# A two-layer decoder trunk on one core: 96 seats in place of 128 in each pass of the expert layer

## The chip, the core and the metric

The kernel runs on 1 core of one Trainium2 chip. The metric is the device time of the whole program, in microseconds (us); lower is better. All inputs and weights are float32 in HBM.

## What is computed

Two decoder layers act on 256 tokens of width 1024. Each has a token mixer (an RWKV-7 group, a short convolution and a dilated attention group behind one projection, then an output projection) and a feed-forward part. The feed-forward part of layer 0 is a dense SwiGLU; that of layer 1 sends each token to 2 of 8 experts of inner width 3584. Cut to what matters here:

```python
SEQ = 256; D_MODEL = 1024; D_FF = 3584; N_EXPERTS = 8; TOP_K = 2
def moe_swiglu(h, router, wg, wu, wd):
    logits = xt @ router
    topv, topi = lax.top_k(logits, TOP_K)
    gates = jax.nn.softmax(topv, axis=-1)
    ...
    # every expert e, for the tokens that chose it:
    #   out[token] += gate * ((silu(x @ wg[e]) * (x @ wu[e])) @ wd[e])
```

## The kernel before, in words

Layer 0, its dense feed-forward part and the mixers of layer 1 come first; the change doesn't touch them. The expert layer is `moe_pass(p)`, which each engine has in its own version: SP (weights), POOL (rows of tokens), PE, ACT and DVE.

**Seats.** Routing gives each token a rank within each of its two experts. A pass has 128 seats for each expert (P = 128): pass 0 serves ranks 0 to 127. DVE sets `flag` when an expert has more tokens than seats (L2468), and each engine ends with a branch on `flag` behind which `moe_pass(1)` stands (L1528 on PE). An empty seat has token 0 and gate 0. At the start of an expert its tokens' rows are gathered from HBM into `x_slots` (L726, POOL, an indirect DMA), turned by eight transposes (`turn_slots`, L1427) and split into a high and a low part, `xg_hi` and `xg_lo`. Expert 0 has a gather by products instead (`gather`, L770).

**Split products.** The products run in float32r, so each float32 product is three: high x high, high x low, low x high (`three`, L789 to L791). The tokens are the stationary operand, 128 rows of the inner dimension by the seats; the weights are the moving operand, 512 columns at a time. Weights arrive by SP's DMAs of 1 MB into a ring of 6 slots. ACT rounds a piece of 1024 columns to `w_hi` (L1543), DVE makes the rest, `w_lo` (L2246); there are four pieces of buffer, and PE frees a piece after six products (`pc_free`).

**Order.** The inner width is walked in 7 chunks of 512 (NJ = 7). For a chunk: gate product into bank 0 or 1 (8 steps of the width), up product into bank 2 or 3 (8 steps), SiLU on ACT (L1911), multiply on DVE (L2505), four transposes on PE (`turn`, L1464), which write bank 6, a copy to `at_hi` on ACT (L1543) and a subtraction to `at_lo` on DVE (L2509), and the down product into banks 4 and 5 (8 steps). That is 24 steps of three products, 72 products a chunk, 7 chunks, 8 experts: 4032 products, 224 transposes of `turn`, and 56 of `turn_slots` for experts 1 to 7. The order is written by hand and fixed: on PE the turn of chunk j - 1 stands between the gate and the up product of chunk j. Experts 0 to 6 are one loop body, expert 7 stands apart. After an expert ACT scales the result by the gates (`yg`, L1940), and POOL adds the rows to `out` in HBM by an indirect DMA (L732); the last expert does so in two halves (L740), and the program ends when the second has landed.

```python
def turn(j, at1):                                     # PE, L1459
    for i in range(4):
        last_ = pe.transpose(bank[6][:, i * P:(i + 1) * P], act_b[j % 2][:, i * P:(i + 1) * P], ident)
```

In a transpose the data are the stationary operand and the identity is the moving one. The mixers' matmuls (L770, L1105) and the transposes are in float32, not float32r.

Of the kernel before, what the change touches and what calls it, by code (L numbers as in the profile page):

```python
# [35 lines left out]
SLOTS = 6  # L36
FIRST_OVER = 4
# [79 lines left out]
def decoder_trunk(nc, x, consts, masks, params, lora, vres_v2, w_in, w_o, dense_wg, dense_wu, dense_wd,  # L117
                  router, gains, moe_wg, moe_wu, moe_wd, h_rows, out):
    with ExitStack() as ctx:
# [29 lines left out]
        xg_hi, xg_lo = (a[:, 0:KT * P] for a in (acts_hi, acts_lo))  # L149
        at_hi, at_lo = (a[:, KT * P:KT * T].rearrange("p (b n) -> p b n", b=2) for a in (acts_hi, acts_lo))  # L150
# [445 lines left out]
        def _(sp):  # L596
# [66 lines left out]
            with sp.If(over_full > 0):  # L663
                moe_pass(1)
# [3 lines left out]
        def _(pool):  # L668
# [52 lines left out]
            def moe_pass(p):  # L721
                def take_rows(e, at1):
                    pool.wait_ge(ga_done, at1 * 2)
                    pool.tensor_copy(from_row[:, :], slot_token[:, e, :]).then_inc(from_set, 1)
                    pool.wait_ge(from_set, at1 - p)
                    pool.indirect_dma_start(x_slots, None, h_rows,  # L726
                                            bass.IndirectOffsetOnAxis(from_row[:, :], 0)).then_inc(slots_in, 16)

                def add_rows(e, at1):
                    pool.wait_ge(to_set, at1 + 1)  # L730
                    pool.wait_ge(yg_kept, at1 * 2 + 2)
                    pool.indirect_dma_start(out, bass.IndirectOffsetOnAxis(to_row[:, :], 0), yg, None,  # L732
                                            compute_op=ALU.add).then_inc(rows_out, 16)
# [12 lines left out]
                pool.wait_ge(index_ready, p + 1)  # L746
                pool.tensor_copy(to_row[:, :], slot_token[:, 0, :]).then_inc(to_set, 1)
                for e in range(NE - 1):
                    take_rows(e + 1, p * NE + e + 1)
                    add_rows(e, p * NE + e)  # L750
                    if e + 2 < NE:
                        pool.tensor_copy(to_row[:, :], slot_token[:, e + 1, :]).then_inc(to_set, 1)
                    else:
                        pool.tensor_copy(to_half[0][:, :], slot_half[:, 0:1])
                        pool.tensor_copy(to_half[1][:, :], slot_half[:, 1:2]).then_inc(to_set, 1)
                add_halves(p * NE + NE - 1)
# [6 lines left out]
            with pool.If(over_full > 0):  # L763
                moe_pass(1)
# [3 lines left out]
        def _(pe):  # L768
# [641 lines left out]
            def moe_pass(p):  # L1410
                def slot_pairs(e):

                    if e == 0:
                        pe.wait_ge(pairs_ready, p + 1)
                    for b in range(2):
                        last_ = mm(bank[7][:, 4 * e:4 * e + 4], onehot[b][:, e, :], token_gate[:, b, e, :],
                                   b == 0, b == 1)
# [12 lines left out]

                def gather(e, at1):

                    for f in range(2):
                        if p == 0:
                            pe.wait_ge(ht_ready, f + 1)
                        for i in range(4):
                            k = 4 * f + i
                            for b in range(2):
                                last_ = mm(bank[1 + 2 * f][:, i * P:(i + 1) * P], h_tok[:, b, k * P:(k + 1) * P],
                                           onehot[b][:, e, :].bitcast(F32) if p else hot_first[:, b, :], b == 0, b == 1)  # L1440
                        last_.then_inc(ga_done, 1)

                def column_chunk(kind, j, at1):
                    if j >= 2:
                        pe.wait_ge(ac_ready, at1 * NJ + (j - 1))
                    b = bank[(0 if kind == "g" else 2) + j % 2]
                    for q in range(4):

                        pe.wait_ge(lo_ready, at1 * PIECES_E + (MOE0 + 4 * place_of[(kind, j)] + q + 1))
                        if kind == "g" and j == 0 and q % 2 == 0:  # L1450
                            pe.wait_ge(ga_low, at1 * 2 + (q // 2 + 1))
                        for i in range(2):
                            k = 2 * q + i
                            ks, cs = slice(k * P, (k + 1) * P), slice(i * CW, (i + 1) * CW)
                            last_ = three(b[:, :], xg_hi[:, ks], xg_lo[:, ks], w_hi[:, q, cs], w_lo[:, q, cs],
                                          k == 0, k == KT - 1)
                        last_.then_inc(pc_free, 1)

                def turn(j, at1):  # L1459
# [3 lines left out]
                    for i in range(4):  # L1463
                        last_ = pe.transpose(bank[6][:, i * P:(i + 1) * P], act_b[j % 2][:, i * P:(i + 1) * P],  # L1464
                                             ident)
                    last_.then_inc(at_done, 1)

                def down_half(j, q, hf):
                    ks, cs = slice(q * P, (q + 1) * P), slice(hf * CW, (hf + 1) * CW)
                    return three(bank[4 + hf][:, :], at_hi[:, j % 2, ks], at_lo[:, j % 2, ks],  # L1470
                                 w_hi[:, q, cs], w_lo[:, q, cs], j == 0 and q == 0, j == NJ - 1 and q == 3)
# [56 lines left out]
            with pe.If(over_full > 0):  # L1528
                moe_pass(1)
# [3 lines left out]
        def _(act):  # L1533
# [366 lines left out]
            def moe_pass(p):  # L1900
                def gathered(at1):
                    for f in range(2):
                        act.wait_ge(ga_done, at1 * 2 + (f + 1))
                        copy(xg_hi[:, f * CW:(f + 1) * CW], bank[1 + 2 * f][:, :]).then_inc(ga_kept, 1)

                def silu(j, at1):
# [4 lines left out]
                    act.activation(sil_b[j % 2], bank[j % 2][:, :], ACT.Silu).then_inc(sl_done, 1)  # L1911

                def turned(j, at1):
                    act.wait_ge(at_done, at1 * NJ + (j + 1))
                    copy(at_hi[:, j % 2, :], bank[6][:, :]).then_inc(at_kept, 1)

                def expert(e, at1, last_one):
# [17 lines left out]
                    for hf in range(2):  # L1935
                        if last_one and hf == 0:
                            act.wait_ge(half_done, p + 1)
                        if last_one and hf:
                            act.wait_ge(pc_free, at1 * PIECES_E + (MOE0 + PIECES_E + PIECES))
                        act.activation(yg[:, hf * 512:(hf + 1) * 512], bank[4 + hf][:, :], ACT.Identity,  # L1940
                                       scale=gate_e).then_inc(yg_kept, 1)
# [19 lines left out]
            with act.If(over_full > 0):  # L1961
                moe_pass(1)
# [4 lines left out]
        def _(dve):  # L1967
# [490 lines left out]
            def finish_ranks():  # L2458
# [9 lines left out]
                TS(flag[:, :], cmax, float(P), None, ALU.is_gt).then_inc(flag_ready, 1)  # L2468
# [15 lines left out]
            def moe_pass(p):  # L2484
# [7 lines left out]
                def gathered(at1, halves_=range(2)):  # L2492
                    for f in halves_:
                        dve.wait_ge(ga_kept, at1 * 2 + (f + 1))
                        fs = slice(f * CW, (f + 1) * CW)
                        TT(xg_lo[:, fs], bank[1 + 2 * f][:, :], xg_hi[:, fs].bitcast(F32), ALU.subtract).then_inc(
                            ga_low, 1)

                def multiply(j, at1):
# [5 lines left out]
                    TT(act_b[j % 2], sil_b[j % 2], bank[2 + j % 2][:, :], ALU.mult).then_inc(ac_ready, 1)  # L2505

                def turned(j, at1):
                    dve.wait_ge(at_kept, at1 * NJ + (j + 1))
                    TT(at_lo[:, j % 2, :], bank[6][:, :], at_hi[:, j % 2, :].bitcast(F32), ALU.subtract).then_inc(  # L2509
                        at_low, 1)  # L2510

                def expert(e, at1, last_one):
# [11 lines left out]
                    dve.tensor_copy(gate_e, slot_gates[:, e, :]).then_inc(gate_ready, 1)  # L2524
# [12 lines left out]
                if p:  # L2537
                    then(TS(rank, rank, -float(P), None, ALU.add))
# [14 lines left out]
                pairs = bank[7][:, 0:4 * NE].rearrange("p (e n) -> p e n", e=NE)  # L2553
                for hf in range(2):
                    TS(slot_half[:, hf:hf + 1], pairs[:, NE - 1, 0:1], 2.0, float(hf), ALU.mult, ALU.add)
                dve.tensor_copy(slot_token[:, :, 0], pairs[:, :, 0]).then_inc(index_ready, 1)
                then(dve.tensor_copy(slot_gates[:, :, 0], pairs[:, :, 1]))
                then(TT(slot_gates[:, :, 0], slot_gates[:, :, 0], pairs[:, :, 2], ALU.add))
# [7 lines left out]
            with dve.If(over_full > 0):  # L2566
                moe_pass(1)
# [48 lines left out]
```

## Time and profile before

| | us |
|---|---|
| median of 3 runs | 1574.8 (1573.14 to 1574.96) |
| span of the profiled execution, first to last instruction | 1570.8 |
| of it before the expert layer's first product (L789 at 612.18) | 612 |
| PE busy / weight loads / DVE / ACT / POOL | 1555.2 / 1360.4 / 1264.9 / 1073.6 / 81.0 |
| read from HBM | 438.63 MB, of it 336 transfers of 1 MB for the experts |
| granted TensorE clock, mean | 0.996 of 2.4 GHz |

The profiled execution's own time is not among the figures; its span is 4.0 us below the median of the runs. PE is matmul time and PEld the weight loads, which lie beside it. Since matmuls are pipelined, the records of two that follow each other overlap; what counts is the distance from start to start.

### The profile page before, as it was taken

The page shows a single profiled execution, that of the slowest core. Times are in us where ns is not written, and L with a number is a line of the kernel's source. Part 1 is how long each engine was busy: PE and PEld are TensorE (multiplying, and loading weights), DVE is VectorE, ACT ScalarE, POOL GpSimd, SP SyncE. Part 2 cuts the span into 40 slices and gives each one's busy share as a digit, 9 for nine tenths or more (in the row PEclk, how much of TensorE's full clock was granted, in tenths as well). Part 3 has the DMA queues.
Part 4 walks back from the last instruction along what each step waited for, and adds up shares of the span by engine and source line. Part 5 has one row for each costly group of instructions (what it writes and reads, how often), then busy time and mean ns, then how long its engine had stood idle before and what let it go on. Part 6 is the DMA issues. An engine that isn't in the chain of part 4 may idle for free.

```text
span 1570.8 us, 28731 instructions
## 1 busy us (share of the span) xinstructions
PE 1555.2 (99%) x10958; PEld 1360.4 (87%) x10958; DVE 1264.9 (81%) x1448; ACT 1073.6 (68%) x1323; POOL 81.0 (5%) x82
## 2 busy tenths in 40 slices
PE   9999999999999999999999999999999999999998
PEld 8989999999999898888888888888888888888886
DVE  5686654444567877999999999999999999999996
ACT  5545444444446455888888888888888888888885
POOL 0022000000000400000000000000000000000000
PEclk9999999999999999999999999999999999999999
DMA  8700655555445008999999999999999999999994
GB/s 314 235 2 3 220 192 180 187 188 185 126 158 158 3 19 321 389 379 360 396 387 348 397 393 359 397 391 354 397 390 353 397 391 356 394 386 366 389 380 162
DMA packets 189944, 447.76 MB, mean 285 GB/s; under 512 B 8208, under 2 KB 10784, under 8 KB 189728
## 3 DMA queue, kind: packets, MB, share of 16 engines
q1 hardware_dynamic: 186480, 434.46, 75.7%
q0 software_dynamic: 2688, 9.44, 2.8%
q10 hardware_dynamic: 688, 2.62, 0.5%
q8 instruction: 63, 1.03, 0.3%
q14 instruction: 25, 0.20, 0.0%
HBM read 438.63 MB, written 6.29 MB: 283 GB/s over the span
## 4 chain that ended last, share of the span: by engine, by line
PE 95%; DVE 3%; ACT 1%; issue 1%; DMA 0%; POOL 0%; SPq 0%; ACTq 0%; DVEq 0%; POOLq 0%
PE bank L789 27%; PE bank L791 27%; PE bank L790 27%; PE bank L770 9%; PE bank L1464 2%; DVE w_lo L2246 1%; ACT w_hi L1543 0%; DMA ring<-in_w_in 0%; PE bank L960 0%; PE bank L810 0%; PE bank L1427 0%; PE bank L1213 0%; PE bank L1105 0%; DVE w_lo L1985 0%; POOL out L740 0%
## 5 line engine op out<-in xcount | busy, mean ns | idle before, releaser
L1543 ACT ACTIVATE w_hi<-ring 128x1024 fp32r<-128x1024 f32 x812 | 858.4, 1061 | 330.1 <-PE bank L791 319.9
L2246 DVE TENSOR_TENSOR w_lo<-ring,w_hi 128x1024 fp32r<-128x1024 f32 x672 | 813.7, 1224 | 60.4 <-ACT w_hi L1543 11.3
L789 PE MATMUL bank<-w_hi,acts_hi 128*128 128x512 f32 (+1 forms) x1376 | 539.0, 392 | 0.4 <-DVE w_lo L2246 0.3
L791 PE MATMUL bank<-w_hi,acts_lo 128*128 128x512 f32 (+1 forms) x1376 | 533.1, 387 | 0.0
L790 PE MATMUL bank<-w_lo,acts_hi 128*128 128x512 f32 (+1 forms) x1376 | 532.3, 387 | 0.0
L791 PEld LDWEIGHTS bank<-w_hi,acts_lo 128*128 128x128 f32 x1376 | 258.3, 188 | 53.7
L789 PEld LDWEIGHTS bank<-w_hi,acts_hi 128*128 128x128 f32 x1376 | 258.6, 188 | 52.1 <-DVE w_lo L2246 1.4
L790 PEld LDWEIGHTS bank<-w_lo,acts_hi 128*128 128x128 f32 x1376 | 258.7, 188 | 50.6
L789 PE MATMUL bank<-acts_hi,w_hi 128*128 128x256 f32 x884 | 252.4, 286 | 1.8 <-DVE acts_lo L2175 0.8
L790 PE MATMUL bank<-acts_lo,w_hi 128*128 128x256 f32 x884 | 250.1, 283 | 0.0
L791 PE MATMUL bank<-acts_hi,w_lo 128*128 128x256 f32 x884 | 250.1, 283 | 0.0
L2237 DVE TENSOR_TENSOR w_lo<-ring,w_hi 128x1024 fp32r<-128x1024 f32 x84 | 102.7, 1225 | 110.8 <-ACT w_hi L1543 110.8
L789 PEld LDWEIGHTS bank<-acts_hi,w_hi 128*128 128x128 f32 x884 | 169.5, 192 | 5.8 <-issue 3.9
L790 PEld LDWEIGHTS bank<-acts_lo,w_hi 128*128 128x128 f32 x884 | 169.6, 192 | 0.0
L791 PEld LDWEIGHTS bank<-acts_hi,w_lo 128*128 128x128 f32 x884 | 169.5, 192 | 0.0
L1985 DVE TENSOR_TENSOR w_lo<-ring,w_hi 128x1024 fp32r<-128x1024 f32 x40 | 48.1, 1220 | 30.9 <-ACT w_hi L1543 30.9
L770 PE MATMUL bank<-arena 64*64 64x128 f32 (+10 forms) x718 | 68.9, 295 | 2.7 <-DVE arena L2452 1.3
L1543 ACT ACTIVATE arena<-bank 128x256 f32<-128x256 f32 (+4 forms) x67 | 30.0, 485 | 57.0 <-PE bank L770 28.4
L770 PEld LDWEIGHTS bank<-arena 64*64 64x64 f32 (+6 forms) x718 | 50.6, 154 | 13.2 <-issue 4.4
L789 PE MATMUL bank<-da_hi,w_hi 128*128 128x256 f32 x192 | 54.3, 283 | 0.0
L790 PE MATMUL bank<-da_lo,w_hi 128*128 128x256 f32 x192 | 54.3, 283 | 0.0
L791 PE MATMUL bank<-da_hi,w_lo 128*128 128x256 f32 x192 | 54.3, 283 | 0.0
(247 smaller groups left out, 1115.9 us busy)
## 6 DMA issues: line engine op xcount, KB each, us to landing
ring<-in_moe_wg SPq DMA_DIRECT2D x112, 1024.0 KB, 6.8
ring<-in_moe_wu SPq DMA_DIRECT2D x112, 1024.0 KB, 7.0
ring<-in_moe_wd SPq DMA_DIRECT2D x112, 1024.0 KB, 6.8
ring<-in_w_in SPq DMA_DIRECT2D x24, 1024.0 KB, 7.5
ring<-in_dense_wg SPq DMA_DIRECT2D x14, 1024.0 KB, 5.2
ring<-in_dense_wu SPq DMA_DIRECT2D x14, 1024.0 KB, 5.2
ring<-in_dense_wd SPq DMA_DIRECT2D x14, 1024.0 KB, 4.9
ring<-in_w_o SPq DMA_DIRECT2D x8, 1024.0 KB, 7.5
```

The costliest lines, as they stand in the source:

```text
L770: return pe.matmul(out_, lhsT, rhs, start=start, stop=stop)
L789: pe.matmul(out_, a_hi, b_hi, start=first, stop=False, **kw)
L790: pe.matmul(out_, a_hi, b_lo, start=False, stop=False, **kw)
L791: return pe.matmul(out_, a_lo, b_hi, start=False, stop=final, **kw)
L1464: last_ = pe.transpose(bank[6][:, i * P:(i + 1) * P], act_b[j % 2][:, i * P:(i + 1) * P], ident)
L1543: return act.activation(o, i, ACT.Copy, **kw)
L1985: TT(w_lo[:, q, :], ring[:, slot_of[n], q % 2 * PIECE:(q % 2 + 1) * PIECE], w_hi[:, q, :].bitcast(F32), ALU.subtract).then_inc(lo_ready, 1)
L2237: TT(w_lo[:, q, :], ring[:, slot_of[n], q % 2 * PIECE:(q % 2 + 1) * PIECE], w_hi[:, q, :].bitcast(F32), ALU.subtract).then_inc(lo_ready, 1)
L2246: TT(w_lo[:, q, :], raw, w_hi[:, q, :].bitcast(F32), ALU.subtract).then_inc(lo_ready, 1)
```

## The change

Seats become 96 (`SEATS`), and `PASSES = -(-256 // 96) = 3`: behind the flag stand passes 1 and 2 in place of pass 1. The threshold of the flag follows. All tiles that have the seats as their free dimension (`xg`, `at`, the transposes' outputs) shrink from 128 to 96 columns a block; those that have them as partitions (`bank` 0 to 5, `sil_b`, `act_b`, `yg`) are used on partitions 0 to 95. POOL gathers and adds 96 rows an expert. The order of the work is the same. Cut to its core (hunks that say the same for another engine or tile are left out):

```diff
+SEATS = 96
+PASSES = -(-T // SEATS)
...
-        xg_hi, xg_lo = (a[:, 0:KT * P] for a in (acts_hi, acts_lo))
+        xg_hi, xg_lo = (a[:, 0:KT * SEATS] for a in (acts_hi, acts_lo))
...
             with pe.If(over_full > 0):
-                moe_pass(1)
+                for p in range(1, PASSES):
+                    moe_pass(p)
...
                     pool.indirect_dma_start(out.rearrange("t (h d) -> (t h) d", h=2),
-                                            bass.IndirectOffsetOnAxis(to_half[hf][:, :], 0),
-                                            yg[:, hf * CW:(hf + 1) * CW], None,
+                                            bass.IndirectOffsetOnAxis(to_half[hf][rows, :], 0),
+                                            yg[rows, hf * CW:(hf + 1) * CW], None,
...
-                            last_ = pe.transpose(bank[1 + 2 * f][:, i * P:(i + 1) * P], x_slots[:, k * P:(k + 1) * P],
-                                                 ident)
+                            last_ = pe.transpose(bank[1 + 2 * f][:, i * SEATS:(i + 1) * SEATS],
+                                                 x_slots[0:SEATS, k * P:(k + 1) * P], ident[0:SEATS, 0:SEATS])
...
-                            ks, cs = slice(k * P, (k + 1) * P), slice(i * CW, (i + 1) * CW)
-                            last_ = three(b[:, :], xg_hi[:, ks], xg_lo[:, ks], w_hi[:, q, cs], w_lo[:, q, cs],
+                            ks, cs = slice(k * SEATS, (k + 1) * SEATS), slice(i * CW, (i + 1) * CW)
+                            last_ = three(b[0:SEATS, :], xg_hi[:, ks], xg_lo[:, ks], w_hi[:, q, cs], w_lo[:, q, cs],
...
-                        last_ = pe.transpose(bank[6][:, i * P:(i + 1) * P], act_b[j % 2][:, i * P:(i + 1) * P],
-                                             ident)
+                        last_ = pe.transpose(bank[6][:, i * SEATS:(i + 1) * SEATS],
+                                             act_b[j % 2][0:SEATS, i * P:(i + 1) * P], ident[0:SEATS, 0:SEATS])
...
-                    copy(at_hi[:, j % 2, :], bank[6][:, :]).then_inc(at_kept, 1)
+                    copy(at_hi[:, j % 2, :], bank[6][:, 0:4 * SEATS]).then_inc(at_kept, 1)
...
-                TS(flag[:, :], cmax, float(P), None, ALU.is_gt).then_inc(flag_ready, 1)
+                TS(flag[:, :], cmax, float(SEATS), None, ALU.is_gt).then_inc(flag_ready, 1)
...
-                    TT(act_b[j % 2], sil_b[j % 2], bank[2 + j % 2][:, :], ALU.mult).then_inc(ac_ready, 1)
+                    TT(act_b[j % 2][0:SEATS, :], sil_b[j % 2][0:SEATS, :], bank[2 + j % 2][0:SEATS, :],
+                       ALU.mult).then_inc(ac_ready, 1)
...
-                    TT(at_lo[:, j % 2, :], bank[6][:, :], at_hi[:, j % 2, :].bitcast(F32), ALU.subtract).then_inc(
+                    TT(at_lo[:, j % 2, :], bank[6][:, 0:4 * SEATS], at_hi[:, j % 2, :].bitcast(F32), ALU.subtract).then_inc(
```

The instructions of the executed path keep their places. The first turn in the expert loop, between a gate and an up product, reads so on PE before (the size is that of the output, partitions by columns):

```order
3678 L791 MATMUL bank<-w_hi,acts_lo 128x512
3679 L1460 ISA
3680 L1464 MATMUL bank<-arena 128x128 x4
3681 L1449 REGISTER_ALU
3682 L789 MATMUL bank<-w_hi,acts_hi 128x512
```

and now:

```order
3678 L797 MATMUL bank<-w_hi,acts_lo 96x512
3679 L1467 ISA
3680 L1471 MATMUL bank<-arena 128x96 x4
3681 L1456 REGISTER_ALU
3682 L795 MATMUL bank<-w_hi,acts_hi 96x512
```

The products keep their 512 columns and lose 32 output partitions; the four transposes lose 32 of 128 columns. PE has 7032 rows in all in place of 5879; all the added ones stand behind the branch on the flag, as the second further pass.

## Rows read from the trace of the kernel before

**Rows 1.** The page: busy time, and the span in 40 slices.

```profile
PE 1555.2 (99%) x10958; PEld 1360.4 (87%) x10958; DVE 1264.9 (81%) x1448; ACT 1073.6 (68%) x1323; POOL 81.0 (5%) x82
...
PEclk9999999999999999999999999999999999999999
```

**Rows 2.** Busy time by stretch (us; x: instructions; then granted clock, DMA share, GB/s).

```profile
135.00:140.00 5.00, 5.00 (x159) 4.87 (x159) 1.90 (x9) 3.46 (x8) 0.00 (x0) 1.00 0.00 0
300.00:400.00 100.00, 100.00 (x836) 100.00 (x835) 49.79 (x44) 42.69 (x44) 0.00 (x0) 1.00 0.55 183
800.00:900.00 100.00, 100.00 (x458) 82.82 (x457) 93.41 (x86) 82.00 (x88) 5.64 (x4) 1.00 1.03 374
```

**Rows 3.** The waits, window 700 to 1500 us: who waited for whom, total, times, longest.

```profile
ACT w_hi L1543 <- PE bank L791: 139.7, 484, 0.4
DVE w_lo L2246 <- ACT w_hi L1543: 9.2, 21, 0.9
```

**Rows 4.** PE in order of time, around the turn at 800 us.

```profile
799.97 0.39 PE L791 MATMUL bank<-w_hi,acts_lo 128*128 128x512 f32 x1
800.20 0.60 PE L1464 MATMUL bank<-arena 128*128 128x128 f32 x4
800.55 0.48 PE L789 MATMUL bank<-w_hi,acts_hi 128*128 128x512 f32 x1
800.87 0.39 PE L790 MATMUL bank<-w_lo,acts_hi 128*128 128x512 f32 x1
...
805.88 0.39 PE L791 MATMUL bank<-w_hi,acts_lo 128*128 128x512 f32 x1
```

**Rows 5.** Groups by form, PE: stationary rows*columns, moving rows x columns, count, busy, mean ns.

```profile
L790 PE MATMUL bank<-w_lo,acts_hi 128*128 128x512 f32 x1344 | 523.2, 389 | 0.0
L790 PE MATMUL bank<-acts_lo,w_hi 128*128 128x256 f32 x884 | 250.1, 283 | 0.0
L1464 PE MATMUL bank<-arena 128*128 128x128 f32 x224 | 33.5, 271 | 0.0
L770 PE MATMUL bank<-arena,ring 128*128 128x256 f32 x128 | 29.3, 383 | 0.0
L1105 PE MATMUL bank<-spare,arena 64*64 64x64 f32 x72 | 3.8, 221 | 0.0
```

**Rows 6.** Groups by form, weight loads of 128 and of 64 columns.

```profile
L790 PEld LDWEIGHTS bank<-w_lo,acts_hi 128*128 128x128 f32 x1376 | 258.7, 188 | 50.6
L1464 PEld LDWEIGHTS bank<-arena 128*128 128x128 f32 x224 | 28.0, 140 | 7.1
L770 PEld LDWEIGHTS bank<-arena 64*64 64x64 f32 x408 | 14.4, 132 | 2.1 <-issue 1.1 <-ACT arena L1543 0.7
```

**Rows 7.** In order of time, start of the expert layer: copy, subtraction, gather.

```profile
608.59 3.84 PE L770 MATMUL bank<-arena 128*128 128x128 f32 x32 [1.29 <-DVE arena L2452]
...
610.68 0.60 ACT L1543 ACTIVATE acts_hi<-bank 128x512 fp32r<-128x512 f32 x1 [2.96 <-PE bank L770]
611.30 0.69 DVE L2496 TENSOR_TENSOR acts_lo<-bank,acts_hi 128x512 fp32r<-128x512 f32 x1 [0.31 <-ACT acts_hi L1543]
...
618.07 0.50 PE L789 MATMUL bank<-w_hi,acts_hi 128*128 128x512 f32 x1 [0.16 <-DVE w_lo L2246]
```

**Rows 8.** Groups of the page: the two splits of a weight piece.

```profile
L1543 ACT ACTIVATE w_hi<-ring 128x1024 fp32r<-128x1024 f32 x812 | 858.4, 1061 | 330.1 <-PE bank L791 319.9
L2246 DVE TENSOR_TENSOR w_lo<-ring,w_hi 128x1024 fp32r<-128x1024 f32 x672 | 813.7, 1224 | 60.4 <-ACT w_hi L1543 11.3
```

**Rows 9.** In order of time, POOL's last issue.

```profile
1564.60 1.55 POOL L740 DMA_INDIRECT out<-arena,to_half  x1 [0.59 <-ACT arena L1940]
```

**Rows 10.** DMA: GB/s in 40 slices, and time to landing of an up half and of the last rows.

```profile
GB/s 314 235 2 3 220 192 180 187 188 185 126 158 158 3 19 321 389 379 360 396 387 348 397 393 359 397 391 354 397 390 353 397 391 356 394 386 366 389 380 162
...
ring<-in_moe_wu SPq DMA_DIRECT2D x112, 1024.0 KB, 7.0
...
out<-arena,to_half POOLq DMA_INDIRECT x2, 4.8
```

More of the change, by code:

```diff
@@ L148, in decoder_trunk @@
         h_hi, h_lo = (a[:, :].rearrange("p (k t) -> p k t", k=KT) for a in (acts_hi, acts_lo))
-        xg_hi, xg_lo = (a[:, 0:KT * P] for a in (acts_hi, acts_lo))
-        at_hi, at_lo = (a[:, KT * P:KT * T].rearrange("p (b n) -> p b n", b=2) for a in (acts_hi, acts_lo))
+        xg_hi, xg_lo = (a[:, 0:KT * SEATS] for a in (acts_hi, acts_lo))
+        at_hi, at_lo = (a[:, KT * P:KT * P + KT * SEATS].rearrange("p (b n) -> p b n", b=2) for a in (acts_hi, acts_lo))
         class Region:
@@ L721, in moe_pass @@
             def moe_pass(p):
+                rows = slice(0, min(SEATS, T - p * SEATS))
                 def take_rows(e, at1):
                     pool.wait_ge(ga_done, at1 * 2)
-                    pool.tensor_copy(from_row[:, :], slot_token[:, e, :]).then_inc(from_set, 1)
+                    pool.tensor_copy(from_row[0:SEATS, :], slot_token[0:SEATS, e, :]).then_inc(from_set, 1)
                     pool.wait_ge(from_set, at1 - p)
-                    pool.indirect_dma_start(x_slots, None, h_rows,
-                                            bass.IndirectOffsetOnAxis(from_row[:, :], 0)).then_inc(slots_in, 16)
+                    pool.indirect_dma_start(x_slots[rows, :], None, h_rows,
+                                            bass.IndirectOffsetOnAxis(from_row[rows, :], 0)).then_inc(slots_in, 16)
                 def add_rows(e, at1):
@@ L731, in add_rows @@
                     pool.wait_ge(yg_kept, at1 * 2 + 2)
-                    pool.indirect_dma_start(out, bass.IndirectOffsetOnAxis(to_row[:, :], 0), yg, None,
+                    pool.indirect_dma_start(out, bass.IndirectOffsetOnAxis(to_row[rows, :], 0), yg[rows, :], None,
                                             compute_op=ALU.add).then_inc(rows_out, 16)
@@ L763, in _ @@
             with pool.If(over_full > 0):
-                moe_pass(1)
+                for p in range(1, PASSES):
+                    moe_pass(p)
         @block.tensor
@@ L1438, in gather @@
                             for b in range(2):
-                                last_ = mm(bank[1 + 2 * f][:, i * P:(i + 1) * P], h_tok[:, b, k * P:(k + 1) * P],
-                                           onehot[b][:, e, :].bitcast(F32) if p else hot_first[:, b, :], b == 0, b == 1)
+                                last_ = mm(bank[1 + 2 * f][:, i * SEATS:(i + 1) * SEATS], h_tok[:, b, k * P:(k + 1) * P],
+                                           onehot[b][:, e, 0:SEATS].bitcast(F32) if p else hot_first[:, b, 0:SEATS],
+                                           b == 0, b == 1)
                         last_.then_inc(ga_done, 1)
@@ L1528, in _ @@
             with pe.If(over_full > 0):
-                moe_pass(1)
+                for p in range(1, PASSES):
+                    moe_pass(p)
         @block.scalar
@@ L1903, in gathered @@
                         act.wait_ge(ga_done, at1 * 2 + (f + 1))
-                        copy(xg_hi[:, f * CW:(f + 1) * CW], bank[1 + 2 * f][:, :]).then_inc(ga_kept, 1)
+                        copy(xg_hi[:, f * 4 * SEATS:(f + 1) * 4 * SEATS], bank[1 + 2 * f][:, 0:4 * SEATS]).then_inc(ga_kept, 1)
                 def silu(j, at1):
@@ L1939, in expert @@
                             act.wait_ge(pc_free, at1 * PIECES_E + (MOE0 + PIECES_E + PIECES))
-                        act.activation(yg[:, hf * 512:(hf + 1) * 512], bank[4 + hf][:, :], ACT.Identity,
-                                       scale=gate_e).then_inc(yg_kept, 1)
+                        act.activation(yg[0:SEATS, hf * 512:(hf + 1) * 512], bank[4 + hf][0:SEATS, :], ACT.Identity,
+                                       scale=gate_e[0:SEATS, :]).then_inc(yg_kept, 1)
                     if not last_one:
@@ L1961, in _ @@
             with act.If(over_full > 0):
-                moe_pass(1)
+                for p in range(1, PASSES):
+                    moe_pass(p)
         @block.vector
@@ L2494, in gathered @@
                         dve.wait_ge(ga_kept, at1 * 2 + (f + 1))
[L2495 to L2496 removed]
+                        fs = slice(f * 4 * SEATS, (f + 1) * 4 * SEATS)
+                        TT(xg_lo[:, fs], bank[1 + 2 * f][:, 0:4 * SEATS], xg_hi[:, fs].bitcast(F32), ALU.subtract).then_inc(
                             ga_low, 1)
@@ L2537, in moe_pass @@
                 if p:
-                    then(TS(rank, rank, -float(P), None, ALU.add))
+                    then(TS(rank, rank, -float(SEATS), None, ALU.add))
                     place_tokens()
@@ L2552, in moe_pass @@
                 dve.wait_ge(pairs_done, p + 1)
-                pairs = bank[7][:, 0:4 * NE].rearrange("p (e n) -> p e n", e=NE)
+                pairs = bank[7][0:SEATS, 0:4 * NE].rearrange("p (e n) -> p e n", e=NE)
                 for hf in range(2):
[L2555 to L2558, printed above, removed]
+                    TS(slot_half[0:SEATS, hf:hf + 1], pairs[:, NE - 1, 0:1], 2.0, float(hf), ALU.mult, ALU.add)
+                seats = slice(0, SEATS)
+                dve.tensor_copy(slot_token[seats, :, 0], pairs[:, :, 0]).then_inc(index_ready, 1)
+                then(dve.tensor_copy(slot_gates[seats, :, 0], pairs[:, :, 1]))
+                then(TT(slot_gates[seats, :, 0], slot_gates[seats, :, 0], pairs[:, :, 2], ALU.add))
                 dve.wait_ge(index_ready, p + 1)
@@ L2566, in _ @@
             with dve.If(over_full > 0):
-                moe_pass(1)
+                for p in range(1, PASSES):
+                    moe_pass(p)
 _OUT = "out"
```

18 lines of the change are left out of this document (9 added, 9 removed).

## The prediction

> **What bounds the kernel now.** I read the page first [rows 1]: PE is busy 99% of the span, the other engines less, and its clock stands at 2.4 GHz but for moments. A busy PE is not yet a PE at its pace, so I next took the stretches [rows 2]: inside the expert layer PE starts 458 matmuls in 100 us, and DVE and ACT are busy 93 and 82 of the 100. Then the waits [rows 3]: in 800 us of expert layer no row has PE waiting for anybody. ACT waits 139.7 us for PE to free a piece of buffer, DVE 9.2 us for ACT. So PE sets the pace, and the splits of the weights follow it.
>
> The order of time around one turn [rows 4] gives PE's own distances. From 800.87 to 805.88 lie 22 steps from start to start, 0.227 us each, of which 512 columns at 2.4 GHz are 213 ns. In the dense part [rows 2] 836 matmuls of 256 columns take 100 us, 120 ns each, of which 107 are columns. Both have 13 to 14 ns beside their columns, a fixed amount. Check: a chunk is 72 products at 0.227 = 16.34 us plus a turn. The turn costs 800.20 to 800.55 for the four transposes, and the second product after it starts 0.32 after the first in place of 0.227: 0.35 + 0.09 = 0.44 us. That is 16.8 us a chunk, 117.5 an expert; with eight transposes of the rows (0.9) 118.4, eight times 947 us, and 612 before it: 1559 of the 1570.8. The rest is the end.
>
> **The change part by part.**
>
> *Does a further pass run?* Only if an expert has over 96 tokens. This is a question of data, not of the profile: the reference's routing of the given inputs puts 53, 55, 65, 74, 56, 60, 86 and 63 tokens on the eight experts. The largest is 86, so the flag stays 0, as with 128 seats, and passes 1 and 2 are code that is skipped by the same single branch as before.
>
> *The 4032 products.* They keep 512 moving columns and lose 32 stationary ones. What shrinks is the weight load: 188 ns for 128 columns, 132 for 64 [rows 6], 0.87 ns a column, so some 160 ns for 96. It was hidden below the 227 ns already, and it stays hidden. The columns' 213 ns stay. Only the fixed 13.6 ns could depend on the stationary columns, and no float32r row of this trace has fewer than 128. The bounds: gone altogether, 4032 x 13.6 = -55 us; in proportion to the columns, 13.6 x 3/4, -3.4 x 4032 = -13.7 us; upwards a third, +4.5 x 4032 = +18 us. I take **0**: the amount is the same with 256 and 512 moving columns and in both parts of the program, which looks like a cost of each matmul, not of what it holds.
>
> *The 224 transposes of turn.* Here the moving operand is the identity, and it shrinks from 128 to 96 columns; the stationary operand, the data, keeps 128 columns and loses 32 rows. What does the distance of 109 ns between two of them hang on ([rows 4]: 0.60 us for four less the last one's 0.271 [rows 5] is 0.329 for three steps)? If on the moving side, it is 128 columns at two cycles of 2.4 GHz, 107 ns. The durations speak for it. Plain float32 matmuls of 64 and 256 moving columns last 221 and 383 ns, 0.84 ns a column, which is two cycles; float32r products of 256 and 512 last 283 and 389, 0.41 ns a column, one cycle [rows 5]. At 128 columns the first line gives 275 ns, the second 230. A transpose lasts 271, so it streams at two cycles. The transposes' loads are also 48 ns shorter than the products' at the same 128 columns, 140 against 188 [rows 6], so a load is not what they wait for. Then 32 columns less are 32 x 0.83 = 26.7 ns each, 107 ns a turn, and **224 x 0.0267 = -6.0 us**. If on the load, it is 0; that is the other bound. I take the first.
>
> A rule bears on this. The Trainium skill, "TensorE: Matmul & The Clock Gate", sections "Back-to-back issue gap" and "LDWEIGHTS (loading the stationary operand)", has a warm matmul cost its moving columns / 2.4 GHz + 2.5 ns, whatever the stationary side, and a load its stationary columns / 1.2 GHz, whatever the rows. By it the products gain nothing, but a transpose would be 56 ns of moving columns behind a load of 107 ns that this change leaves alone, so the -6.0 and the -1.5 below would be 0; it is the first rival.
>
> *The 56 transposes of the rows* (turn_slots) are the same form, 8 for each of experts 1 to 7: 56 x 0.0267 = **-1.5 us**, bound 0. All these lie in PE's own line, where nobody else is waited for, so each ns comes off the end.
>
> *The first gather* is 32 matmuls in 3.84 us [rows 7], some 0.115 us apart, more than 107 of moving columns at two cycles: by load, which stays. 0; bound -0.8 us (32 x 26.7 ns).
>
> *Copies and subtractions.* ACT's copy of turned data takes 0.60 us for 512 columns against 1.06 for 1024 [rows 7, 8], 0.90 ns a column; 128 fewer save 0.12. DVE's subtraction: 0.69 against 1.22, 1.04 ns a column, saves 0.13. In mid-layer they lie beside PE, whose waits are nil [rows 3]; they are worth 0 there and make the splits' room a little wider. At the start PE does wait for them: the first product needs copy and subtraction, and at 618.07 PE waits for DVE, whose line holds two subtractions. 0.12 + 2 x 0.13 = **-0.4 us**. At the last chunk PE waits for DVE again, behind ACT's copy: **-0.1 us**. SiLU, multiply and the scaling work on fewer partitions but the same 512 columns; 0.
>
> *The end.* The last thing is POOL's issue of the second half of the last rows, 1.55 us [rows 9], and its landing, 4.8 us [rows 10], both for 128 rows. If the issue scales with rows, 96 save 0.39; if it is fixed, 0. The landing in proportion would save 1.2, fixed 0. I take **-0.4** for both. The other gathers and adds lie behind 107 us of an expert; 0.
>
> *The weights.* PE goes from 118.4 to 117.4 us an expert (7 x 0.107 + 8 x 0.027). The transfers then need 44.04 MB in 117.4 us, 375 GB/s over 372. Slices with 397 stand in the trace [rows 10], an up half lands after 7.0 us where a slot's turn of six is over 16 us, so nothing becomes late. DVE's 93 of 100 becomes about 93.6: it is next in line but not reached.
>
> **Sum**: -6.0 - 1.5 - 0.4 - 0.1 - 0.4 = -8.4 us, 1562.4 of span. The span is 4.0 below the median of the runs, and what lies around it doesn't change: 1574.8 - 8.4 = **1566.4 us**, 0.5% faster.
>
> **The rivals.**
>
> 1. *The transposes wait for their loads*, 128 stationary columns before and after. For it: 109 ns is also what 128 columns at 0.83 ns take, and two explanations fit one number. Against it: the two-cycle duration, the shorter load of 140 ns, and the gather, which is load-bound and slower at 0.115. Then only -0.9 remains: 1573.9, not to be told from no change.
>
> 2. *The fixed 13.6 ns shrink with the stationary columns*, to three quarters: a further -13.7 us, 1552.7. For it: the trace doesn't say what they are, and a handing over of 128 columns would fit. Against it: nothing direct. A small part of it, 1 ns a product, would already be -4 us.
>
> 3. *Slower: the step from one stationary set to the next gets longer when the set isn't a full 128 columns.* Its place is the start of each of the 4032 products. It decides from 8.4 / 4032 = 2.1 ns a product on; if the 13.6 ns rise by a third, +18 us gives 1584.5. Against it: the float32 matmuls on 64 stationary columns lie on one line of duration with those on 128 [rows 5], the transposes too, and the 160 ns load has 67 ns of room. The Trainium skill, same page, section "Weight-path perf modes", says that the fast weight load is on only with exactly 128 weights and a type other than float32, which would be lost at 96. The products' loads show no fast mode that could be lost: the 64 columns between 132 and 188 ns take 0.87 ns each, one cycle of 1.2 GHz.
>
> 4. *A further pass runs after all*, if the routing on the chip gave an expert over 96 tokens: from 612 to the end is a pass of 950 us, so over 2500 us. With 86 tokens at most, it would need ten tokens to change expert.
>
> 5. *The clock falls*, since three quarters of the array's columns work. The stretch of 64x64 matmuls at 135 us, a quarter of the array, was granted 1.00 [rows 2]. A chance too small to count.
>
> **How the numbers follow.** A measurement of this kernel can tell about 0.2%, 3.1 us, from no change. Forecast 0.65, with a range of its own from 1563 to 1569 (landing and gather at either bound, a few tenths of a ns on the products); rival 1 0.13; rival 2 0.13, some of it as a small part; rival 3 0.08; rivals 4 and 5 together 0.01. Faster: 0.65 + 0.13 = 0.78; same 0.13; slower 0.09. The range holds the forecast, rival 1 up to 1575 and the part of rival 2 up to 1.3 ns a product (another -5.4 us): **1561 to 1575**. It leaves out the rest of rival 2 and all of 3 and 4.
>
> **What the changed profile would show.** Four transposes in 0.49 us in place of 0.60, and each lasting about 244 ns in place of 271. Products still 0.227 apart, with loads of some 160 ns. A chunk of 16.7 us. No row of PE waits inside the layer. The copy at 0.48 and the subtraction at 0.55 us. POOL's last issue at 1.2 to 1.55 us. Products at another distance than 0.227 by over 1 ns make the prediction wrong, in either direction; so do transposes still 109 ns apart.

## The result, and the profile after

| | us |
|---|---|
| before, median of 5 runs | 1574.8 (1572.98 to 1575.24) |
| changed kernel, median of 5 runs | 1580.13 (1579.69 to 1583.82) |
| ratio over all runs, 95% interval | 1.0044 (1.0031 to 1.0057) |
| span of the profiled executions, before and after | 1570.8, 1581.3 |
| forecast | 1566.4 (1561 to 1575) |

The kernel became slower: the median rose by 5.3 us (0.34%), and the ratio, which is taken over all runs and not from the two medians, is 1.0044 (0.44%), where 0.5% faster was forecast. The profiled execution was the slowest of the five (1583.82), with the granted clock at 0.59 of full speed from 608 to 616 us, at the first gather; the spans of the other four are 1577.3 to 1579.5.

The page of the changed kernel, busy time and weight loads, answering to [rows 1] and [rows 8]:

```profile
PE 1565.2 (99%) x10958; PEld 1249.5 (79%) x10958; DVE 1256.0 (79%) x1448; ACT 1065.7 (67%) x1323; POOL 83.6 (5%) x82
...
L2255 DVE TENSOR_TENSOR w_lo<-ring,w_hi 128x1024 fp32r<-128x1024 f32 x672 | 814.5, 1223 | 77.6 <-ACT w_hi L1551 60.9
```

PE runs the same 10958 instructions: no further pass ran. Weight loads take 111 us less, DVE and ACT 8 to 9 less, PE 10 more. The stretch 900 to 1000 us, first of the kernel before, then of the changed one (columns as in [rows 2]):

```profile
900.00:1000.00 100.00, 100.00 (x458) 82.82 (x457) 93.39 (x87) 81.94 (x88) 4.21 (x4) 1.00 1.04 381
```

```profile
900.00:1000.00 100.00, 100.00 (x454) 70.38 (x453) 91.41 (x85) 80.51 (x87) 4.40 (x4) 1.00 1.03 372
```

454 matmuls in place of 458, at the full clock in both. DVE and the transfers are less busy, so neither has become the bound. The waits of the changed kernel, 700 to 1500 us, against [rows 3]:

```profile
ACT w_hi L1551 <- PE bank L797: 152.7, 480, 0.4
...
DVE w_lo L2255 <- ACT w_hi L1551: 54.2, 292, 0.9
```

Again no row has PE waiting. ACT waits longer for PE, and DVE longer for ACT: all follow a slower PE. PE in order of time at a turn, against [rows 4]:

```profile
803.70 0.39 PE L797 MATMUL bank<-w_hi,acts_lo 128*96 128x512 f32 x1
803.93 0.49 PE L1471 MATMUL bank<-arena 96*128 96x96 f32 x4
804.21 0.45 PE L795 MATMUL bank<-w_hi,acts_hi 128*96 128x512 f32 x1
804.50 0.39 PE L796 MATMUL bank<-w_lo,acts_hi 128*96 128x512 f32 x1
...
806.12 0.40 PE L797 MATMUL bank<-w_hi,acts_lo 128*96 128x512 f32 x1
```

The four transposes take 0.49 us, as forecast. But from 804.50 to 806.12 there are seven steps of 0.231 us, where the kernel before has 0.227. Single distances tell more. In the kernel before, the distance after the first product of a turn is about 316 ns, the next nine or so are 224 to 236, and then they settle to a strict 227, 226, 227. In the changed kernel they never settle; they go on, nearly all between 228 and 236. Over some 3300 distances between products from 700 to 1500 us, without the long one after each turn, the mean is 227.3 before and 231.5 after.

That closes the account. An expert, from its first row transpose to that of the next, took 118.57 us and takes 119.71, 1.14 more. Its 504 products cost 504 x 4.2 = +2.1; its seven turns, 0.67 us before and 0.57 now from the first transpose to the second product, give back 0.7, and the eight row transposes 0.2, together 1.2. The first expert, from its first product to the row transposes of the next, takes 114.9 us in both traces: +2.0 for its 480 products, less 0.7 for its turns, 0.4 for a wait near 618 us that is gone, and 0.7 for a group of 16 small matmuls near 624 us. The other seven take 7.9 us more, and the end is 0.3 shorter: +7.6 us. The other 2.9 of the 10.5 us between the two spans stand before the first product, 2.8 of them at the first gather, where the clock fell in this execution and not in that of the kernel before. The medians differ by less, 5.3, since four of the five runs of the changed kernel had mean clocks of 0.997 and 0.998. The 35 runs of the kernel before that were timed beside the experiments had 0.995 as their median, and from 0.998 to 0.994 their time rises by 1.2 us for each 0.001. At 0.998 the three runs of the changed kernel, 1579.7 to 1580.1 us, stand 8 us above the one run of the kernel before, 1571.5.

### The profile page after: what moved, and what is told of

Same layout as the page of the kernel before. It is cut to its first block, busy times and chain, and to the rows that moved or that the text cites. A ratio compares the mean times of both kernels' runs of the same rounds, so it can differ in the third digit from the quotient of the medians.

```text
span 1581.3 us, 28731 instructions
## 1 busy us (share of the span) xinstructions
PE 1565.2 (99%) x10958; PEld 1249.5 (79%) x10958; DVE 1256.0 (79%) x1448; ACT 1065.7 (67%) x1323; POOL 83.6 (5%) x82
## 4 chain that ended last, share of the span: by engine, by line
PE 96%; DVE 2%; ACT 1%; issue 1%; DMA 0%; POOL 0%; SPq 0%; DVEq 0%; ACTq 0%; POOLq 0%
PE bank L795 28%; PE bank L797 28%; PE bank L796 27%; PE bank L776 9%; PE bank L1471 1%; ACT w_hi L1551 0%; DMA ring<-in_w_in 0%; PE bank L966 0%; PE bank L816 0%; PE bank L1433 0%; PE bank L1219 0%; DVE w_lo L1994 0%; PE bank L1111 0%; POOL out L745 0%; ACT arena L1551 0%
## 5 line engine op out<-in xcount | busy, mean ns | idle before, releaser
L795 PE MATMUL bank<-w_hi,acts_hi 128*96 128x512 f32 (+1 forms) x1376 | 541.4, 393 | 0.2 <-DVE w_lo L2255 0.2
L797 PE MATMUL bank<-w_hi,acts_lo 128*96 128x512 f32 (+1 forms) x1376 | 539.4, 392 | 0.0
L796 PE MATMUL bank<-w_lo,acts_hi 128*96 128x512 f32 (+1 forms) x1376 | 536.4, 390 | 0.0
L797 PEld LDWEIGHTS bank<-w_hi,acts_lo 128*96 128x96 f32 (+1 forms) x1376 | 222.8, 162 | 94.1
L796 PEld LDWEIGHTS bank<-w_lo,acts_hi 128*96 128x96 f32 (+1 forms) x1376 | 223.5, 162 | 90.9
L795 PEld LDWEIGHTS bank<-w_hi,acts_hi 128*96 128x96 f32 (+1 forms) x1376 | 223.0, 162 | 89.6 <-DVE w_lo L2255 1.0
L796 PE MATMUL bank<-acts_lo,w_hi 128*128 128x256 f32 x884 | 250.1, 283 | 0.0
L796 PEld LDWEIGHTS bank<-acts_lo,w_hi 128*128 128x128 f32 x884 | 169.6, 192 | 0.0
L776 PE MATMUL bank<-arena 64*64 64x128 f32 (+11 forms) x718 | 72.0, 300 | 3.2 <-DVE arena L2461 1.3
L796 PE MATMUL bank<-da_lo,w_hi 128*128 128x256 f32 x192 | 54.3, 283 | 0.0
```

The costliest lines, as they stand in the source:

```text
L776: return pe.matmul(out_, lhsT, rhs, start=start, stop=stop)
L795: pe.matmul(out_, a_hi, b_hi, start=first, stop=False, **kw)
L796: pe.matmul(out_, a_hi, b_lo, start=False, stop=False, **kw)
L797: return pe.matmul(out_, a_lo, b_hi, start=False, stop=final, **kw)
```

## The experiments

The theories: A, the distance of the products depends on how many columns the stationary operand has; B, the short transposes keep PE out of step; C, it is where the blocks begin, every 96 columns (384 bytes) in place of 128.

**e1_wide_loads.** The changed kernel with blocks 128 columns apart, of which 96 are seats and 32 hold leftovers, and products on all 128. Cut to the gate and up products; the down product changes likewise, and the copies and subtractions write their 96 columns into the wider blocks:

```diff
-                            ks, cs = slice(k * SEATS, (k + 1) * SEATS), slice(i * CW, (i + 1) * CW)
-                            last_ = three(b[0:SEATS, :], xg_hi[:, ks], xg_lo[:, ks], w_hi[:, q, cs], w_lo[:, q, cs],
+                            ks, cs = slice(k * P, (k + 1) * P), slice(i * CW, (i + 1) * CW)
+                            last_ = three(b[:, :], xg_hi[:, ks], xg_lo[:, ks], w_hi[:, q, cs], w_lo[:, q, cs],
```

Expected: 

> The change, but the products' stationary operand has 128 columns again (96 seats and 32 columns of leftovers, blocks 128 apart); transposes, copies and subtractions stay at 96. Theory A (the products' distance depends on the number of stationary columns): products 0.227 apart as before, transposes 82 ns apart, so 7.5 to 9 us below before, 1566 us, ratio 0.995. Theory B (the shorter transposes, or the rows left out in them, keep PE out of step afterwards): products stay 231.5 ns apart, about 1580 us. Theory C (where the blocks begin, every 384 bytes in the change): 0.227 here too; the next run tells C from A.

Measured: 1568.96 us (1564.51 to 1570.23), ratio 0.9965 (0.9952 to 0.9979). Mean distance of the products 227.1, and 82 ns from transpose to transpose. Theory B falls: the short transposes are all there, and the products settle again. PE in order of time, and the stretch 900 to 1000 us:

```profile
830.38 0.40 PE L805 MATMUL bank<-w_hi,acts_lo 128*128 128x512 f32 x1
830.61 0.49 PE L1479 MATMUL bank<-arena 96*128 96x96 f32 x4
830.89 0.47 PE L803 MATMUL bank<-w_hi,acts_hi 128*128 128x512 f32 x1
831.21 0.39 PE L804 MATMUL bank<-w_lo,acts_hi 128*128 128x512 f32 x1
```

```profile
900.00:1000.00 100.00, 100.00 (x461) 82.82 (x460) 93.12 (x87) 81.61 (x87) 3.37 (x4) 1.00 1.04 380
```

461 matmuls in 100 us. The turn is 0.59 us in the mean, against 0.67 before and 0.57 in the changed kernel. An expert takes 117.75 us, against 118.57 before.

**e2_held96, e2_held64, e2_held112, e6_held127.** The kernel before, where only the products' stationary columns are cut; HELD is 96, 64, 112, 127. Seats from HELD on are left out of the products; with 64 some of these hold tokens. The output partitions shrink with the stationary columns, so no run tells the two apart. Cut to the gate and up products, the down product changes likewise:

```diff
-                            ks, cs = slice(k * P, (k + 1) * P), slice(i * CW, (i + 1) * CW)
-                            last_ = three(b[:, :], xg_hi[:, ks], xg_lo[:, ks], w_hi[:, q, cs], w_lo[:, q, cs],
+                            ks, cs = slice(k * P, k * P + HELD), slice(i * CW, (i + 1) * CW)
+                            last_ = three(b[0:HELD, :], xg_hi[:, ks], xg_lo[:, ks], w_hi[:, q, cs], w_lo[:, q, cs],
```

Expected of 96: 

> The kernel before, with 96 of the 128 columns of each block as the products' stationary operand and 96 output partitions; all else as before, blocks 128 columns apart, transposes of 128. Seats 96 to 127, which are empty, are left out of the products. Theory A: products 231.5 ns apart, 4.2 ns x 4032 = 17 us slower, 1592 us, ratio 1.011. Theories B and C: 227 ns and 1575 us, no change.

Expected of 64: 

> As the last, with 64 stationary columns; seats from 64 on are left out of the products. Theory A has two forms. If any number below 128 puts PE out of step: 231 to 232 ns, span near 1587. If the cost grows with the columns missing: 4.2 ns for 32 is 8.4 for 64, 235.7 ns, span near 1605. Theories B and C: 227 ns.

Expected of 112: 

> As the last, with 112 stationary columns; seats 112 to 127, which are empty, are left out. Theory A, any number below 128: 231 to 232 ns, span near 1587. Theory A, in proportion: 2.1 ns more, 229.4 ns, span near 1579. Theories B and C: 227 ns.

Expected of 127: 

> The kernel before with 127 of 128 stationary columns in the products; seat 127, which is empty, is left out. Theory A as a step at 128: 230 to 231 ns between products, as with 112, 96 and 64, span near 1583. Theory A in proportion: 227.3 ns, span near 1571.

| stationary columns | mean distance, ns | weight load, ns | an expert, us | span, us |
|---|---|---|---|---|
| 64 | 229.9 | 134 | 119.89 | 1580.7 |
| 96 | 230.0 | 161 | 119.88 | 1586.6 |
| 112 | 230.4 | 175 | 120.06 | 1584.0 |
| 127 | 233.4 | 187 | 121.51 | 1596.4 |
| 128 (before) | 227.3 | 188 | 118.57 | 1570.8 |

Only the kernel with 96 was timed more than once: 1584.52 us (1582.35 to 1588.36), ratio 1.0059 (1.0043 to 1.0075). Its clock was 0.994 in the profiled execution, hence the span above that with 112. Theory A holds, as a step at 128 and not in proportion: one column less than 128 costs 6 ns a product, 16 less cost 3.1, 32 or 64 less 2.7. Never settling isn't what costs the time: with 127 columns the products do settle, to a strict 233, 233, 234. The stretch 900 to 1000 us with 96 and with 127, and the weight loads of 127 and of 64 columns, grouped by form, 700 to 1500 us:

```profile
900.00:1000.00 100.00, 100.00 (x453) 71.01 (x452) 92.45 (x86) 81.11 (x87) 3.73 (x4) 1.00 1.03 376
```

```profile
900.00:1000.00 100.00, 100.00 (x448) 80.51 (x447) 91.33 (x84) 80.18 (x86) 4.08 (x4) 1.00 1.02 370
```

```profile
L791 PEld LDWEIGHTS bank<-w_lo,acts_hi 128*127 128x127 f32 x1106 | 207.0, 187 | 48.8
```

```profile
L791 PEld LDWEIGHTS bank<-w_lo,acts_hi 128*64 128x64 f32 x1121 | 150.7, 134 | 101.0
```

453 matmuls with 96 columns and 448 with 127. The load's own record knows no step: 134, 161, 175, 187, 188 ns is a straight line of 0.84 ns a column. The products' records do know it. Their durations grow nearly as much as their distances; the same product, by its mean duration (the last number but one) with 128, with 96 in the changed kernel, and with 127, 700 to 1500 us:

```profile
L790 PE MATMUL bank<-w_lo,acts_hi 128*128 128x512 f32 x1134 | 441.5, 389 | 0.0
```

```profile
L796 PE MATMUL bank<-w_lo,acts_hi 128*96 128x512 f32 x1123 | 440.6, 392 | 0.0
```

```profile
L791 PE MATMUL bank<-w_lo,acts_hi 128*127 128x512 f32 x1107 | 437.3, 395 | 0.0
```

**e3_apart.** e1_wide_loads with 96 stationary columns in the products; that is, the changed kernel with its blocks 128 apart.

```diff
-        xg_hi, xg_lo = (a[:, 0:KT * SEATS] for a in (acts_hi, acts_lo))
+        xg_hi, xg_lo = (a[:, 0:KT * P] for a in (acts_hi, acts_lo))
...
-                            ks, cs = slice(k * SEATS, (k + 1) * SEATS), slice(i * CW, (i + 1) * CW)
+                            ks, cs = slice(k * P, k * P + SEATS), slice(i * CW, (i + 1) * CW)
```

Expected: 

> The change with its blocks 128 columns apart, as before, in place of 96: products on 96 stationary columns, transposes of 96. Against e1_wide_loads only the number of stationary columns of the products differs. Theory A (number of columns) with the spacing of blocks of no account: products 231.5 ns apart as in the change, 1580 us, ratio 1.004. If the spacing of the blocks makes the 1.5 ns between the change (231.5) and the kernel before with 96 columns (230.0): 230.0 ns and about 1574 us. If the short transposes make it: 231.5 ns.

Measured: 1577.16 us (1573.56 to 1578.62), ratio 1.0009 (0.9999 to 1.0018), not to be told from the kernel before. The mean distance is 230.0 ns, as in e2_held96, and an expert takes 118.95 us against 119.71. The stretch 900 to 1000 us:

```profile
900.00:1000.00 100.00, 100.00 (x457) 70.76 (x456) 92.03 (x86) 80.95 (x87) 5.46 (x4) 1.00 1.03 374
```

So theory C has a share: of the 4.2 ns, 2.7 come with the number of columns and 1.5 with blocks that begin every 384 bytes. Whether the distance between blocks or where each begins matters wasn't tried.

**e4_seats88 and e5_seats68.** e1_wide_loads with fewer seats, `SEATS = 88`, and `SEATS = 68` with the flag's threshold left at 128, so that seats from 68 on, some of which hold tokens, are left out and no further pass runs.

Expected of 88: 

> e1_wide_loads with 88 seats: the largest expert has 86 tokens, so no further pass runs. Products on 128 columns 227 ns apart. If the transposes go by moving columns, 88 x 0.83 + 2 = 75 ns apart against 82, 280 x 6.7 ns = 1.9 us less than e1_wide_loads, about 1567 us, ratio 0.995. If their load has become the limit: 82 ns, no gain.

Expected of 68: 

> e1_wide_loads with 68 seats and the flag's threshold left at 128; seats from 68 on are left out. If the transposes still go by moving columns: 68 x 0.83 + 2 = 58.7 ns apart, span 280 x 23.3 ns = 6.5 us below e1_wide_loads. If the load of 128 columns (some 58 ns of its 140, from the 48 ns by which it is shorter than the products') takes over: 60 to 65 ns. If it is a load of 107 ns, it could not be below that, which the 82 ns of the change exclude already.

Measured: with 88 seats 1569.12 us (1567.85 to 1570.94), ratio 0.9966 (0.9953 to 0.9978), transposes 75 ns apart; with 68, a single run of 1574.86 us, transposes 62 ns apart. PE in order of time, first with 88, then with 68:

```profile
835.91 0.47 PE L1479 MATMUL bank<-arena 88*128 88x88 f32 x4
```

```profile
835.37 0.41 PE L1479 MATMUL bank<-arena 68*128 68x68 f32 x4
```

Down to 88 columns the transposes go by their moving columns (109, 82, 75 ns for 128, 96, 88; every third or so is 4 ns longer with 96 and 88). At 68 it would be 58.7 and is 62, and the next product starts 43 ns after the last transpose in place of 28, so something else, perhaps the load, begins to count. The measured times don't fall with it, but the length of an expert does, which repeats to 0.01 us in most experts of a trace: 117.75 us with 96 seats in three traces, 117.57 with 88 (here and in e8_wide_gather88), mostly 117.21 with 68. For 88 that is 0.18 x 8 = 1.4 us, an estimate that the times can't confirm. Both profiled executions had the clock at half for 10 us from 608 us on, and the mean clock was 0.993 to 0.995 in all runs of e4_seats88, 0.991 in that of e5_seats68.

**e7_wide_gather, e1_again, e8_wide_gather88, before_again.** Does the narrower first gather bring the clock down? Cut to the gather itself; the first copies and subtractions read its blocks 128 apart:

```diff
-                                last_ = mm(bank[1 + 2 * f][:, i * SEATS:(i + 1) * SEATS], h_tok[:, b, k * P:(k + 1) * P],
-                                           onehot[b][:, e, 0:SEATS].bitcast(F32) if p else hot_first[:, b, 0:SEATS],
+                                n = SEATS if p else P
+                                last_ = mm(bank[1 + 2 * f][:, i * n:(i + 1) * n], h_tok[:, b, k * P:(k + 1) * P],
+                                           onehot[b][:, e, 0:SEATS].bitcast(F32) if p else hot_first[:, b, :],
```

Expected of the wide gather: 

> e1_wide_loads, with the 32 matmuls of the first gather on 128 moving columns again. Theory D (the clock falls at the first gather, near 608 us, because fewer columns stream there): no fall there in this profile, mean granted clock 0.996 to 0.998 in most runs, median 1566 to 1567. Theory N (the fall there is chance): the same spread of clock and time as e1_wide_loads, median 1569.

Expected of e1 again: 

> e1_wide_loads once more, beside the run with the wide gather. Both theories: median near 1569, products 227 ns and transposes 82 ns apart. Theory D: a fall of the clock near 608 us in this profile; theory N: either.

Expected of 88 seats: 

> 88 seats, products on 128 columns, the first gather on 128 moving columns. Theory D: no fall near 608 us, 1.9 us below e7_wide_gather, about 1565, ratio 0.9935. Theory N: as e4_seats88, 1567 to 1569, clock 0.994 to 0.997.

Expected of before: 

> The kernel before once more, for a second profile. Theory D: no fall of the clock near 608 us. Theory N: one may show.

| | median us | ratio (95%) | granted clock of the runs |
|---|---|---|---|
| e7_wide_gather | 1568.09 | 0.9960 (0.9946 to 0.9974) | 0.994 to 0.997 |
| e1_again | 1566.67 | 0.9952 (0.9938 to 0.9966) | 0.995 to 0.998 |
| e8_wide_gather88 | 1566.86 | 0.9957 (0.9942 to 0.9973) | 0.994 to 0.997 |
| before_again (one run) | 1575.9 | | 0.994 |

The stretch 608 to 616 us, of before_again and of e7_wide_gather:

```profile
608.00:616.00 8.00, 6.71 (x40) 6.22 (x40) 6.03 (x15) 2.21 (x4) 0.00 (x0) 0.79 0.15 56
```

```profile
608.00:616.00 8.00, 7.17 (x36) 7.05 (x37) 5.22 (x17) 0.98 (x2) 0.00 (x0) 0.58 0.01 6
```

The clock fell there with the wide gather too, and in a second execution of the kernel before, and didn't in the first execution of e1_wide_loads. So theory D falls as it was put: the fall at the router and first gather comes and goes. Over all 14 profiles it came in 5 of 6 with the narrow gather and in 4 of 8 with the wide one, too few to say that the narrow one doesn't make it likelier. From the start of the gather to the first product it costs 1.6 us in before_again and 2.8 in the changed kernel (5.23 and 6.35 us against 3.59). It isn't the only fall that comes and goes: the clock was also at half for some us near 430 us in all 14 profiles and near 181 us in 11 of them (not in e1_wide_loads, whose mean clock was 0.998). Since the clock blurs 2 us, the times leave the worth of 88 seats over 96 open.

## Why the prediction was wrong

- **What bounds the kernel**: right. PE's own distances set the pace before and after; no row of PE waits, DVE and the transfers stayed behind. DVE was forecast to be busier, 93.6 of 100; it is at 91.4, since PE is slower, and waits for ACT 54 us in place of 9, which costs nothing.
- **No further pass** (rival 4): right, the counts of instructions agree. **No fall of the clock** through fewer columns (rival 5): right, the stretch from 900 to 1000 us has 1.00 in both.
- **The 4032 products, "I take 0"**: the step that failed. It was +4.2 ns a product, 17 us: 2.7 for fewer than 128 stationary columns, 1.5 for blocks every 384 bytes. My reason was that the fixed 13.6 ns were alike with 256 and 512 moving columns and in both parts of the program. Those rows all have 128 stationary columns and blocks that begin at multiples of 512 bytes. They vary two things that the change leaves alone and hold fixed the two that it moves, so they couldn't carry a 0. The upper bound of +18 us, taken from a rise by a third, was met almost exactly. That is luck, since no row gave the third; it got a chance of 0.08 and stood outside the range.
- **The 224 and 56 transposes, -7.5 us**: the mechanism was right, the size a little high. They went from 109 to 82 ns apart, so a load of 107 ns, as rival 1 had it, is not behind each. But four transposes have three distances between them; the step from the last to the next product stayed at 28 ns. In e1_wide_loads a turn is 0.08 us shorter and not 0.107, eight row transposes 0.18: -4.4 and -1.3 us. The products settle after seven steps there in place of ten, which gives another 0.1 us an expert, so that an expert takes 117.75 us, 0.82 less than before and not 1.0. In the changed kernel a turn is 0.105 us shorter, as forecast, but by luck: only 0.08 of it lies between the transposes, and 0.03 in the step from the first product to the second, 286 ns in place of 316, which the forecast left alone. That step is short in e3_apart too, and about 314 in e1_wide_loads and e2_held96; why isn't shown.
- **Start and end, -0.9 us**: most of it came. PE's wait at 618 us is gone in e1_wide_loads, worth 0.4 with the slower product behind it, but the way from the gather's start to the first product is 3.60 us there and 3.59 before, and at the last chunk PE waits for DVE 0.17 us against 0.18. POOL's last issue takes 1.42 us in place of 1.55, and from the last product's start to the end of the span it is 7.3 in place of 7.6 us. The first gather, put at 0, takes 3.81 in place of 3.84. One term was left out: 16 matmuls of the routing near 624 us, with 4 moving columns and the seats as stationary columns, stand in PE's line too. They are 85 ns apart in place of 112, and with the step before them that is 0.7 us in the changed kernel.
- **Rival 3**, slower from 2.1 ns a product on, is what happened. I argued against it with float32 matmuls on 64 stationary columns, whose durations lie on one line with the others. Those are other forms in another type, and the line was too coarse: I let 271 ns pass for the 275 of the line, a gap as large as the whole effect. The change raised the products' duration from 389 to 392 ns (L790, now L796) and their distance by 4.2. No row of the trace before held float32r products on fewer columns, as the prediction itself says. The other argument was the load, and its records lie on a straight line through 127 and 128, while the distances jump by 6 ns. The rule of the Trainium skill ("TensorE: Matmul & The Clock Gate", "Weight-path perf modes"), that exactly 128 stationary columns of a type other than float32 get a faster load, has its step just where the runs show one. Whether it is this load that makes the step isn't shown: its records show no fast form, 188 ns for 128 columns and 187 for 127, and the rule doesn't tell why 127 columns cost more than 96. I took that for a refutation, and it was none.
- **Rival 1** and **rival 2** are excluded by 82 ns between transposes and by 231.5 between products. The gap that I quoted from the Trainium skill beside rival 1 is what its section "Back-to-back issue gap" gives for a single matmul; for pairs of load and matmul that section has both set the distance, with 131 ns at 512 columns, and here it is 227.3.

What stays open is what in PE makes the step at 128, whether it goes with the stationary columns or with the output partitions, why 127 is worse than 112, and why 384-byte blocks cost 1.5 ns.

The best version is e1_wide_loads: the transposes, copies and rows shrink to 96 seats, the products keep 128 columns. Twice timed, 1568.96 and 1566.67 us against 1574.5 to 1574.7, ratios 0.9965 and 0.9952: faster than the kernel before by 0.4 to 0.5%, and than the change, which was not timed beside it, by 0.7 to 0.9%.

## What to carry to other kernels

Shrink what streams, and leave the stationary operand of a float32r product at its full 128 columns, even if a quarter of them holds leftovers, with blocks at full spacing. In this kernel, whose 4032 products stand one behind the other, that was worth 11 to 13 us against the version that shrank everything. Where a term is a few ns times thousands of instructions, "fixed" must be tested against the dimension that the change moves; if no row of the trace varies that dimension, its bounds belong into the range.

## What the runs showed of the hardware

- Products of 512 moving columns at 2.4 GHz, weights loaded anew each time: 227.3 ns apart on 128 stationary columns, 233.4 on 127, 230.4 on 112, 230.0 on 96, 229.9 on 64. The loads themselves take 0.84 ns a column, 134 to 188 ns, and are shorter than the distance in all of these.
- The same products on 96 columns are 231.5 ns apart if the blocks begin every 384 bytes, 230.0 if every 512.
- Matmuls of 4 moving columns, weights loaded anew each time, are 112 ns apart on 128 stationary columns and 85 on 96 (near 624 us): 0.84 ns a stationary column. There the distance goes by the stationary side.
- After four transposes, products on 128 columns need seven steps (transposes of 96 columns) to ten (128) until they settle into 227, 226, 227 ns.
- float32 transposes are 109, 82 and 75 ns apart for 128, 96 and 88 moving columns, 0.84 ns a column or two cycles of 2.4 GHz, then 62 for 68.
- The clock fell to half near 608 us for some us in one execution of the kernel before and not in another (mean clock 0.79 and 1.00 from 608 to 616 us), after 12 matmuls with 8 moving columns and a wait of 1.3 us; over 35 runs of that kernel each 0.001 of mean clock goes with some 1.2 us of time.
